# Two changes of order: where GpSimd begins the adding transfers of the first mixer, and where product 2's weight pairs are put

## What is computed

```
# block 1
h = rms_norm(x, ln_pre_mix);  proj = h @ w_in        # 256 pool columns, q, k, v of 12 heads
mix = concat([multi_scale_pool(u), dilated_attention(rope(q), rope(k), v)]) @ w_out
x = x + rms_norm(mix, ln_post_mix)
h = rms_norm(x, ln_pre_ffn)
x = x + rms_norm((silu(h @ w_gate) * (h @ w_up)) @ w_down, ln_post_ffn)
# block 2
z = rms_norm(x, ln_mix_2) @ w_in_2                    # three kinds of attention
x = x + concat([o_a, o_b, o_c]) @ w_out_2
u = rms_norm(x, ln_ffn_2) @ w_up_2;  c = causal_conv(u);  gate, val = split(c)
x = x + (silu(gate) * val) @ w_down_2                 # w_down_2: 2816 x 1024
x = x + (p_2 @ w_ple_proj_2) * sigmoid(rms_norm(x, ln_ple_2) @ w_ple_gate_2)
```

## Time and profile before

| what | us |
|---|---|
| median of three runs | 1270.86 (1270.75 to 1271.94) |
| the profiled execution | 1271.55 |
| its span, first to last instruction | 1269.7 |
| TensorE matmuls busy in the span | 1254.5 (99%) |
| VectorE, ScalarE, GpSimd busy | 947.2, 729.3, 510.5 |

### The profile page before, as it was taken

How to read it: one execution, slowest core, us unless ns; L and a number is a source line. 1 busy time by engine, 2 the same in 40 slices (tenths; PEclk the granted TensorE clock), 3 DMA queues, 4 the chain that set the end, 5 groups by cost and what they waited for, 6 DMA issues and landing times.

```text
span 1269.7 us, 22055 instructions
## 1 busy us (share of the span) xinstructions
PE 1254.5 (99%) x7684; PEld 1141.8 (90%) x7684; DVE 947.2 (75%) x1732; ACT 729.3 (57%) x1437; POOL 510.5 (40%) x578
## 2 busy tenths in 40 slices
PE   8999999999999999999999999999999999999998
PEld 7999978999999988889999999889889999787887
DVE  6687766799888878884566778457987777789754
ACT  5666744545555556646667788445455555556452
POOL 5676781256556401036788866310122323000000
PEclk9999999999999999999999999999999999999999
DMA  7799833343333376444597943132323232564121
GB/s 231 224 201 225 181 92 102 98 132 101 99 105 116 109 257 185 131 132 151 144 244 146 172 93 116 68 120 83 100 84 109 90 112 70 207 233 166 68 99 67
DMA packets 145607, 173.45 MB, mean 137 GB/s; under 512 B 25420, under 2 KB 111643, under 8 KB 145522
## 3 DMA queue, kind: packets, MB, share of 16 engines
q1 hardware_dynamic: 129600, 145.15, 35.6%
q0 software_dynamic: 15920, 27.18, 12.1%
q10 hardware_dynamic: 2, 0.00, 0.0%
HBM read 170.22 MB, written 39.85 MB: 165 GB/s over the span
## 4 chain that ended last, share of the span: by engine, by line
PE 88%; DVE 6%; POOL 2%; ACT 2%; issue 1%; DMA 1%; ACTq 0%; SPq 0%; DVEq 0%; POOLq 0%
PE ps L2833 13%; PE ps L2834 13%; PE ps L2835 13%; PE ps L2952 6%; PE ps L2959 6%; PE ps L2954 6%; PE ps L3085 3%; PE ps L3089 3%; PE ps L3087 3%; PE ps L3129 3%; PE ps L3131 3%; PE ps L3130 3%; PE ps L3047 2%; PE ps L3035 2%; PE ps L3036 2%; DVE w_lo L2382 1%
## 5 line engine op out<-in xcount | busy, mean ns | idle before, releaser
L2833 PE MATMUL ps<-h_hi,w_hi 128*128 128x256 f32 (+1 forms) x748 | 238.2, 318 | 0.0
L2834 PE MATMUL ps<-h_lo,w_hi 128*128 128x256 f32 (+1 forms) x748 | 237.4, 317 | 0.0
L2835 PE MATMUL ps<-h_hi,w_lo 128*128 128x256 f32 (+1 forms) x748 | 237.2, 317 | 0.0
L2952 PE MATMUL ps<-w_hi,h_hi 128*128 128x384 f32 (+2 forms) x512 | 162.6, 328 | 0.0
L2954 PE MATMUL ps<-w_hi,h_lo 128*128 128x384 f32 (+2 forms) x512 | 157.9, 319 | 0.0
L2835 PEld LDWEIGHTS ps<-h_hi,w_lo 128*128 128x128 f32 x748 | 142.5, 191 | 9.6
L2833 PEld LDWEIGHTS ps<-h_hi,w_hi 128*128 128x128 f32 x748 | 142.6, 191 | 9.2 <-DVE h_lo L2129 0.3
L2834 PEld LDWEIGHTS ps<-h_lo,w_hi 128*128 128x128 f32 x748 | 142.6, 191 | 8.4
L1273 POOL TENSOR_TENSOR w_lo<-w_raw,w_hi 128x384 fp32r<-128x384 f32 (+2 forms) x114 | 120.7, 1133 | 26.4 <-ACT w_hi L1513 26.3
L2959 PE MATMUL ps<-w_lo,h_hi 128*128 128x384 f32 (+2 forms) x512 | 101.9, 319 | 0.7 <-DVE w_lo L2290 0.7
L3129 PE MATMUL ps<-w_hi,st_hi 128*128 128x512 f32 x252 | 98.8, 392 | 2.2 <-DVE st_lo L2393 1.8
(11 more groups left out here) (327 smaller groups left out, 3332.8 us busy)
## 6 DMA issues: line engine op xcount, KB each, us to landing
w_raw<-in_w_up_dram SPq DMA_DIRECT2D x25, 1024.0 KB, 5.4
w_raw<-in_w_in_dram SPq DMA_DIRECT2D x69, 256.0 KB, 4.8
w_raw<-in_w_gate_dram SPq DMA_DIRECT2D x11, 1024.0 KB, 5.4
down_sums<-in_w_down_dram SPq DMA_DIRECT2D x18, 512.0 KB, 5.4
down_sums<-in_w_down_dram SPq DMA_DIRECT2D x36, 256.0 KB, 6.2
down_sums<-in_w_down_dram POOLq DMA_DIRECT2D x12, 768.0 KB, 9.2
down_sums<-down_sums POOLq DMA_DIRECT2D x12, 768.0 KB, 9.2
w_raw<-in_w_out_dram SPq DMA_DIRECT2D x8, 1024.0 KB, 5.1
```

Source lines behind the costliest of these rows:

```text
L2833: pe.matmul(out_, s_hi, m_hi, start=first and n == 0, stop=False, skip_group_check=True)
L2834: pe.matmul(out_, s_hi, m_lo, start=False, stop=False, skip_group_check=True)
L2835: mm = pe.matmul(out_, s_lo, m_hi, start=False, stop=last and n == len(pairs) - 1, skip_group_check=True)
L2952: pe.matmul(bank, h_hi[:, kb0 + i, tok], hi[:, i, :], start=half == 0 and i == 0, stop=False, skip_group_check=True)
```

## The change

Two things. In the first mixer the twelve adding DMAs are begun behind low parts of projection weights instead of behind normalisations: `ADD_AFTER[0]` now counts the low parts that GpSimd has made in that mixer. And in product 2 (d = 1 only; product 1 keeps its places) step i goes into raw place i mod 6. So steps 2 to 5 are the first in the places of `h_raw`, and their loads wait for the last gate part and the last value half (`gate_part`, `val_part`); step 6 is the first to take a place again, that of step 0, and waits for step 0's low parts and `first_sums_lo`.

```diff
-ADD_AFTER = ((9, 12, 15, 18, 20, 23, 25, 27, 29, 32, 35, 38), (8, 11, 14, 17, 20, 23, 26, 29, 32, 35, 38, 41))
+ADD_AFTER = ((21, 23, 25, 27, 29, 31, 33, 37, 39, 41, 45, 49), (8, 11, 14, 17, 20, 23, 26, 29, 32, 35, 38, 41))
...
-def down_place(i):
-    return (1, 0, 2, 3, 4, 5)[(i - 1) % 6] if i else 0
+def down_place(d, i):
+    return i % 6 if d else (1, 0, 2, 3, 4, 5)[(i - 1) % 6] if i else 0
...
                 for i in range(STEPS):
-                    src, earlier = rows(w)[i % STRASSEN], before_in_place(i)
+                    src, earlier = rows(w)[i % STRASSEN], before_in_place(d, i)
                     if i < 2:
                         for sem_, value in slots_free[i]:
                             sp.wait_ge(sem_, value)
+                    elif earlier is None and d:
+                        sp.wait_ge(gate_part, SEVEN * N_MIXED)
+                        sp.wait_ge(val_part, 2 * N_MIXED)
                     elif earlier is None:
                         sp.wait_ge(down_part, part_at(d, 0, "P6"))
                     else:
                         sp.wait_ge(down_lo, weights_lo_at(d, earlier + 1, 0))
                         if d and not earlier:
                             sp.wait_ge(first_sums_lo, 1)
...
                 for n in range(PLAIN):
-                    last = max(i for i in range(STEPS) if down_place(i) == n)
+                    last = max(i for i in range(STEPS) if down_place(d, i) == n)
                     sp.wait_ge(down_lo, weights_lo_at(d, last + 1, 0))
...
                     if kind == "split_lo":
                         weights_lo(mx, s[1], s[2])
+                        split_pieces += 1
+                        if mx.b == 0 and split_pieces in ADD_AFTER[0]:
+                            sums_added(0, *ADD_ORDER[ADD_AFTER[0].index(split_pieces)])
...
-                        if normed_units in ADD_AFTER[mx.b]:
-                            sums_added(mx.b, *ADD_ORDER[ADD_AFTER[mx.b].index(normed_units)])
+                        if mx.b and normed_units in ADD_AFTER[1]:
+                            sums_added(1, *ADD_ORDER[ADD_AFTER[1].index(normed_units)])
```

More of the change, by code:

```diff
@@ L95, in quarters_free, with before_in_place @@
     return max(part_at(d, i - 2, name) for name in order_of(d, i - 2) if table[name] in quarters)
-def down_place(i):
-    return (1, 0, 2, 3, 4, 5)[(i - 1) % 6] if i else 0
-def before_in_place(i):
-    earlier = [n for n in range(i) if down_place(n) == down_place(i)]
+def down_place(d, i):
+    return i % 6 if d else (1, 0, 2, 3, 4, 5)[(i - 1) % 6] if i else 0
+def before_in_place(d, i):
+    earlier = [n for n in range(i) if down_place(d, n) == down_place(d, i)]
     return earlier[-1] if earlier else None
@@ L125, in raw_at @@
 def raw_at(d, i):
-    same = [n for n in range(STEPS) if down_place(n) == down_place(i)]
-    return 32 * sum(1 for e in range(d + 1) for n in same if e < d or n <= i)
+    place = down_place(d, i)
+    return 32 * sum(1 for e in range(d + 1) for n in range(STEPS) if down_place(e, n) == place and (e < d or n <= i))
 def round_done(j, k=SEVEN):
@@ L1006, in features, with down_raw_of @@
             return slice(KH * half, KH * half + KH)
-        def down_raw_of(i):
-            n = down_place(i)
+        def down_raw_of(d, i):
+            n = down_place(d, i)
             if n < 2:
@@ L1029, in down_piece, with down_source @@
             return w[:, down_slot(i), 512 * first:512 * end]
-        def down_source(i, name):
+        def down_source(d, i, name):
             first, end = W_PIECES[name]
-            return down_raw_of(i)[:, first:end, :].rearrange("p k n -> p (k n)")
+            return down_raw_of(d, i)[:, first:end, :].rearrange("p k n -> p (k n)")
         def row_quarters(st, i, first, end):
@@ L1090, in down_loads @@
                             sp.wait_ge(first_sums_lo, 1)
-                    dst, done = down_raw_of(i), down_raw[down_place(i)]
+                    dst, done = down_raw_of(d, i), down_raw[down_place(d, i)]
                     j = i % STRASSEN
@@ L1277, in mixer @@
                 own_n, own_d = mx.cnt.of[mx.steps[0]]["N"], 0
-                normed_units = 0
+                normed_units = split_pieces = 0
                 for s in mx.orders["pool"]:
@@ L1387, in first_sums_low @@
                 pool.wait_ge(down_hi, weights_hi_at(1, 0, count))
-                return pool.tensor_tensor(down_piece(w_lo, 0, name), down_source(0, name),
+                return pool.tensor_tensor(down_piece(w_lo, 0, name), down_source(1, 0, name),
                                           down_piece(w_hi, 0, name).bitcast(F32), ALU.subtract)
@@ L1667, in down_high @@
             def down_high(d, i, name):
-                act.wait_ge(down_raw[down_place(i)], raw_at(d, i))
+                act.wait_ge(down_raw[down_place(d, i)], raw_at(d, i))
                 if i >= 2:
                     act.wait_ge(down_part, quarters_free(d, i, W_QUARTER, range(*W_PIECES[name])))
-                act.activation(down_piece(w_hi, i, name), down_source(i, name), ACT.Copy)\
+                act.activation(down_piece(w_hi, i, name), down_source(d, i, name), ACT.Copy)\
                     .then_inc(down_hi, 2 if name in ("BT", "T24") else 1)
@@ L2381, in down_low @@
                 dve.wait_ge(down_hi, weights_hi_at(d, i, {"B11": 1, "T1": 2, "BT": 2, "T24": 4, "B2": 1, "T3": 2}[name]))
-                dve.tensor_tensor(down_piece(w_lo, i, name), down_source(i, name), down_piece(w_hi, i, name).bitcast(F32),
+                dve.tensor_tensor(down_piece(w_lo, i, name), down_source(d, i, name), down_piece(w_hi, i, name).bitcast(F32),
                                   ALU.subtract).then_inc(down_lo, 2 if name == "BT" else 1)
```

## The result

The changed kernel takes **1276.45 us** in the median of five runs (1275.62 to 1278.97); the kernel before took 1270.86 beside it. The ratio is 1.0041, with a 95% interval of 1.003 to 1.0051: slower by 5 us, where 3.3 us less was forecast. The profiled execution took 1275.62 us with a span of 1273.9, 4.2 us more than that of before.

A forecast was written before the change was run, and what follows sets the result against it. TensorE, busy 1254.5 of 1269.7 us, was taken to bound the kernel, so only its gaps could gain. 1.14 us (first mixer) plus 2.2 (product 2) made 3.3 us less: 1267.5 us, range 1266.7 to 1269.9.

The forecast's parts named there:

- Product 2: At step 2 of product 2: its load begins 1.7 us earlier, so TensorE regains 2.2 us (1.7 to 2.4).
- the sum: Adds 1.14 us in the first mixer and 2.2 in product 2, to 3.3 us less on TensorE.
- T2 and T4 of group 2: First mixer: both begun earlier, GpSimd's wait before T4 goes and TensorE's gap near 169 shrinks from 1.24 to 0.10: 1.14 us.
- The other ten adds at 0: First mixer: the other adds start 2 to 20 us earlier, and GpSimd's idle time makes up the delay: 0 us.
- 10.2 us: Landing time of group 2's last copy after its begin at about 109.76, giving 120.0; the middle copy takes 6.2 us.
- Us for us: In the third rival, TensorE stalls one us for each us of copy landing from 119.7 on.
- a lock of GpSimd by VectorE: VectorE may block GpSimd's descriptor writes through their shared port: an estimated 2.5 us on a begin that meets it.
- The third: Rival: GpSimd is held at low part 37 by group 2's copies; slower, 1274.6 us at a 17 us landing; chance 0.05.
- Fewer adds run beside the copies: Reason given against the third rival, that group 2's copies hold GpSimd at low part 37.

The follow-up runs named there:

- the two runs with only the second wait: Changed kernel, T1 of group 1 behind low part 31: 1277.31 us; new raw places, old add places, T1 of group 2 behind low part 37: 1272.36 us.
- run with one add at 37: Kernel before with the new raw places of product 2 and only T1 of group 2 moved, behind low part 37: 1272.36 us, ratio 1.0003.
- the run that keeps this wait alone: Changed kernel with T1 of group 2 behind low part 41 instead of 37, T1 of group 1 still behind 27: 1269.04 us, ratio 0.9979.
- first wait later: Changed kernel with T1 of group 1 behind low part 31 instead of 27, T1 of group 2 still behind 37: 1277.31 us, ratio 1.0043.
- twelve memsets: Kernel before with twelve chained GpSimd memsets in front of low part 38 of mixer 1: 1273.52 us, ratio 1.0015.
- twenty memsets: Kernel before with twenty chained GpSimd memsets in front of low part 38 of mixer 1: 1276.77 us, ratio 1.0043.
- the adds alone: Kernel before with only mixer 1's adds moved behind low parts, product 2 keeping its raw places: 1281.2 us, ratio 1.0069.

## Why the prediction was wrong

**Product 2: right.** Step 2's load began with the last value half, landed in 4.7 us (forecast: nearer to 4.8 than to 6.8), and TensorE had no gap at step 2. The gain was put at 2.2 (1.7 to 2.4); the traces give 2.5, the runs of this half alone 3.1 (1.9 to 4.2). Some 0.2 us of that came at the later gaps of steps 8 and 9, which the sum had named and not counted.

**T2 and T4 of group 2: right by itself.** GpSimd's wait in front of the last add is gone from the changed kernel, and so is TensorE's gap near 169; 1.13 us of offset come back there against 1.14 forecast. The run that moves T2 of group 2 and no other add bears it out in the trace.

**The other ten adds at 0: wrong, and this is the whole miss.** Four things failed in it, in this order.
1. *The copies' begin was taken as fixed at 109.76.* Only their landing was given a range. But the adds brought forward use the same DMA engines, which were already full there (a share of 1.04 to 1.19, over 1 as the profile counts it, from 100 to 118 in the kernel before), and SyncE's rows of issues between 90 and 117, 0.5 to 2.7 us long before, grew to as much as 7.64 us. From 108 to 112 GpSimd's queue took 89.5% of the DMA engines' time and SyncE's 22.1%; before it was 59.3% and 45.0%. The last copies began at 116.39 and landed fast, in 5.4 us. The sentence that 10.2 us "were measured beside adds that now come before 100 us" took this for relief; those adds were what pushed the copies back. In the two runs with only the second wait, which differ ahead of the copies in the adds of groups 0 and 1 alone, the last copies began at 115.76 and at 108.81.
2. *The first reader behind the wait was the wrong one.* I followed the queue to low part 40, which TensorE reads at 125.3. The map in the middle of that queue is wanted 3 us sooner: by the rows after, TensorE transposes 3.34 us behind the end of GpSimd's wait (123.40 to 126.74), and it wanted to at 122.28. The landing from which TensorE stalls is thus 118.9, not 119.7. The forecast's own landing of 120.0 was already past it. (The run with one add at 37, where the wait ended at 118.79, has no stall for the map.)
3. *"Us for us" was wrong.* The stall cost its own 3.72 us, 2.58 of low clock, and then came 1.3 at a wait on VectorE, with GpSimd's new rhythm. The clock's part was seen again with plain memsets.
4. *An order of GpSimd's own instructions was priced at nothing.* It is not: where GpSimd's tensor operations follow each other closely, VectorE's sum of two SBUF tiles waits for several of them (3.22, 4.35, 4.67 us). I had weighed the shared port only for a lock of GpSimd by VectorE, and that stayed without effect: the twelve begins took up to 2.42 us, but the next instruction followed 0.8 to 0.9 us behind each. The other direction decided. "SBUF — State Buffer", section "SBUF: two separate sides", of the Trainium skill has it too: a VectorE operation with two SBUF inputs and a GpSimd operation that reads SBUF exclude each other for a whole instruction. The traces agree, and show more: the sum of 4.35 us waited for three GpSimd tensor operations in a row.

T1 of group 1, behind low part 27, was not costed at all. GpSimd stood 5.84 us there, more than at any place that I examined; that it cost nothing is luck, shown by the run that keeps this wait alone.

**The rivals.** The third was the one that came, with its place and its mechanism, at a chance of 0.05. By its own formula a landing at 123.4 gives 1267.5 + 3.7 = 1271.2; what its price lacked is points 2 to 4. "Fewer adds run beside the copies", the reason against it, was point 1 again.

**Left open.** Why SyncE's issues take longer when the DMA engines are full was not tried by itself. What sets the length of the low clock, which pauses of GpSimd let VectorE's sum through, and 2.1 us of the run with one add at 37 are open too.

## What to carry to other kernels

When transfers are begun earlier, ask which transfers they now stand in front of: a begin time read from the trace of before holds only as long as what shares its DMA engines stays behind it. Behind a new wait, list everything queued on that engine and take the earliest reader, not the last; a stall of TensorE of 3.6 to 5 us may be charged some 1.5 to 2.6 us more for the clock, as it was in four traces here. The order of GpSimd's instructions is a resource too: VectorE's two-input operations wait while its tensor operations follow each other closely, and one pause in the right place was worth 1 us of TensorE's time here.

## What the runs showed of the hardware

- A DMA issue on SyncE's queue is not a fixed cost: 0.52 and 1.19 us for the first copy of a pair in the kernel before (94.15, 107.91), 4.93 to 8.40 us for such a copy in five runs with more adds begun ahead of it, and the loads behind it on that queue wait.
- While GpSimd stood for the copies, the DMA engines ran dry: a share of 0.02 in 122 to 124, against 1.08 in the kernel before, because the next load waited for GpSimd's low part. A wait on a transfer ended by starving the transfers.
- The price of a stall in clock isn't in proportion to its length. A stall of 3.57 us was followed by about 6 us at a granted clock of 0.50, one of 4.96 us (first wait later) by about 3, a gap of 1.83 us (twelve memsets) by about 3 as well; one of 2.77 us (twenty memsets, at 178.21) and those of 1.24 and 1.30 us left it at 1.00. By the offset up to the next transposition the low clock cost 2.6 us in the changed kernel and with twenty memsets, 1.6 with the adds alone, 1.5 with the first wait later.
